# First two pairs of the up projection without the seven-product scheme, and another order of reads in its last pair

## What is computed

```
m = rmsnorm(h, g_mlp)
h = h + square(relu(m @ w_up)) @ w_down        # 1024 -> 4096 -> 1024
```

## Time and profile before

| | us |
|---|---|
| median of 3 runs | 4737.99 (4730.15 to 4739.12) |
| time of the profiled execution | 4743.6 |
| its span, first to last instruction | 4741.8 |
| PE busy in it | 4288.3 |
| first up phase, from its first load to pair 2 | 77.8 |
| second up phase, the same stretch | 78.9 |

### The profile page before, as it was taken

The page is one execution under the profiler, slowest core; times in us unless marked ns, Lnnn a source line. Parts: engine busy times, 40 slices in busy tenths (PEclk is TensorE's granted clock), DMA queues, the critical chain, the costliest instruction groups (busy, mean ns, idle before and its releaser), DMA issues. The chain is left out here.

```text
span 4741.8 us, 67334 instructions
## 1 busy us (share of the span) xinstructions
PE 4288.3 (90%) x28381; PEld 3484.5 (73%) x28381; DVE 2114.8 (45%) x2906; ACT 1598.6 (34%) x2680; POOL 633.2 (13%) x514
## 2 busy tenths in 40 slices
PE   7988899987979979899998799999989778899998
PEld 5988889756958858677435588788767676787887
DVE  4544426363245552324443566433442363765333
ACT  3632234342243332311675333222332333433221
POOL 0024400010001100002231232000100002221001
PEclk8999999998989989999999899999999898999999
DMA  3110012122110021111001132431111211234222
GB/s 111 38 60 2 2 45 67 47 64 80 44 36 9 9 75 48 63 40 45 32 9 31 55 111 107 143 97 58 53 33 42 65 40 42 92 112 151 82 91 71
DMA packets 320899, 284.92 MB, mean 60 GB/s; under 512 B 19505, under 2 KB 286033, under 8 KB 320482
## 3 DMA queue, kind: packets, MB, share of 16 engines
q1 hardware_dynamic: 320610, 280.76, 19.0%
HBM read 204.55 MB, written 55.31 MB: 55 GB/s over the span
## 5 line engine op out<-in xcount | busy, mean ns | idle before, releaser
L3063 PE MATMUL ff_bank<-ff_x_hi_rounded,ff_wh_rounded 128*128 128x512 f32 x896 | 361.3, 403 | 56.8 <-DVE ff_wl_rounded L3226 37.3
L3081 PE MATMUL ff_acc<-ff_x_hi_rounded,ff_wh_rounded 128*128 128x512 f32 x1024 | 398.3, 389 | 0.0
L3081 PE MATMUL ff_acc<-ff_x_hi_rounded,ff_wl_rounded 128*128 128x512 f32 x1024 | 398.3, 389 | 0.0
L3081 PE MATMUL ff_acc<-ff_x_rounded,ff_wh_rounded 128*128 128x512 f32 x1024 | 398.3, 389 | 0.0
L3063 PE MATMUL ff_bank<-ff_x_hi_rounded,ff_wl_rounded 128*128 128x512 f32 x896 | 357.8, 399 | 0.0
L3063 PE MATMUL ff_bank<-ff_x_rounded,ff_wh_rounded 128*128 128x512 f32 x896 | 357.2, 399 | 0.0
L3063 PEld LDWEIGHTS ff_bank<-ff_x_hi_rounded,ff_wh_rounded 128*128 128x128 f32 x896 | 173.6, 194 | 106.1 <-DVE ff_wl_rounded L3226 45.5
L3125 ACT ACTIVATE ff_wh_rounded<-ff_wl 128x512 fp32r<-128x512 f32 x128 | 80.8, 632 | 418.8 <-DMA ff_wl<-w_down_dram 208.2
L3081 PEld LDWEIGHTS ff_acc<-ff_x_rounded,ff_wh_rounded 128*128 128x128 f32 x1024 | 192.2, 188 | 40.1
L3081 PEld LDWEIGHTS ff_acc<-ff_x_hi_rounded,ff_wh_rounded 128*128 128x128 f32 x1024 | 192.2, 188 | 40.0
L3081 PEld LDWEIGHTS ff_acc<-ff_x_hi_rounded,ff_wl_rounded 128*128 128x128 f32 x1024 | 192.2, 188 | 39.6
(11 more groups left out here) (623 smaller groups left out, 10421.7 us busy)
## 6 DMA issues: line engine op xcount, KB each, us to landing
inner<-ff_made_out SPq DMA_DIRECT2D x64, 512.0 KB, 2.6
ff_x<-inner SPq DMA_DIRECT2D x64, 512.0 KB, 5.5
ff_raw<-w_up_dram SPq DMA_DIRECT2D x32, 512.0 KB, 4.1
ff_wl<-w_down_dram SPq DMA_DIRECT2D x64, 256.0 KB, 3.1
ff_raw<-w_mlp_dram SPq DMA_DIRECT2D x32, 512.0 KB, 4.2
ff_wl<-w_mlp_dram SPq DMA_DIRECT2D x64, 256.0 KB, 3.0
mid_w<-w_in_dram SPq DMA_DIRECT2D x104, 128.0 KB, 2.6
pa_w<-w_in_dram SPq DMA_DIRECT2D x72, 128.0 KB, 2.6
```

The source lines that it names most:

```text
L3063: mm = M(to, rounded(a[:, j, h, :]), rounded(b[:, j, h, :]), start=(j in (0, 1, 5) and h == 0 and i == 0), stop=(h == H - 1 and i == 2), s ...
L3081: mm = M(acc[:, s, c, :], rounded(a[:, s, k, :]), rounded(b[:, at, c * W2:(c + 1) * W2]), start=(k == 0 and i == 0), stop=(k == KD - 1 and ...
```

## The change

Pairs 0 and 1 (`PLAIN` = 2) are made in the ordinary form: four steps `u`, each one weight block against two input blocks of 512 tokens, 24 matmuls, so 96 matmuls a pair instead of 84. They need no combinations, so POOL leaves `combine(0)` and `combine(1)` out, and the input blocks 0, 1, 5 and 6 alone: ACT writes each high part straight from `hid` with the gain, 1024 elements at once, and DVE makes the low part from `hid` in one instruction. The first pair's weights come in four DMAs of 256 KB instead of two of 512 KB. The four combinations are made during pairs 0 and 1, from scaled copies that `scale_x` writes: blocks 4, 2 and 3 by POOL in nine subtractions (eight of 512 elements, then one of 2048), block 1 by DVE in one of 2048 (`t3`, which lies in `square`). They are split (`high_t`, `low_t`) at the start of pair 2, the first in the seven-product form. In the last pair `read(LAST, 1)` and `read(LAST, 2)` come ahead of `high_y(0)` on ACT, and DVE's reads and `shape` are placed differently among its `low_y`.

```diff
--- before.py
+++ after.py
...
+    PLAIN, SLOT = 2, (0, 5, 6, 3)
...
+        t3 = square[:, :, :].rearrange("p s (h n) -> p (s h) n", n=W2)
+        products = lambda q: 4 * min(q, PLAIN) + J * max(q - PLAIN, 0)
+        act_reads = lambda q: 2 * min(q, PLAIN) + 4 * max(q - PLAIN, 0)
+        dve_reads, sums_made = lambda q: 3 * max(q - PLAIN, 0), lambda q: 4 * max(q - PLAIN, 0)
+        first_half = lambda q: 0 if q < PLAIN else 1
+        plain_acc = {(0, 0): acc[:, 1], (0, 1): bank[:, 0:2], (1, 0): bank[:, 2:4], (1, 1): acc[:, 0]}
...
+                cols = q * 2 * P
+                if q == 0:
+                    for u in range(4):
+                        ks, f = slice(u % 2 * H, (u % 2 + 1) * H), u // 2
+                        sp.dma_start(raw[:, ks, f * P:(f + 1) * P], up_view[:, ks, f * P:(f + 1) * P]).then_inc(raw_first[u], 16)
+                    return
+                if q <= PLAIN:
+                    sp.wait_ge(w_low, products(q))
+                else:
+                    sp.wait_ge(w_low, products(q - 1) + 6)
+                    sp.wait_ge(combined, sums_made(q))
...
+                store(q, first_half(q))
                 if q + 2 < PAIRS:
                     load_pair(q + 2)
-                store(q, 0)
+                store(q, 1 - first_half(q))
...
+            def multiply_plain(q, u):
+                to, j, blocks = plain_acc[q, u // 2], SLOT[u], (0, 1) if u % 2 == 0 else (5, 6)
+                pe.wait_ge(w_low, products(q) + u + 1)
+                if (q, u) == (1, 2):
+                    pe.wait_ge(act_read, 1)
+                for h in range(H):
+                    if q == 0 and u < 2:
+                        pe.wait_ge(x_low, u * H + h + 1)
+                    for c in range(C2):
+                        for i, (a, b) in enumerate(((wh, x_hi), (wl, x_hi), (wh, x))):
+                            mm = M(to[:, c, :], rounded(a[:, j, h, :]), rounded(b[:, blocks[c], h, :]),
+                                   start=(u % 2 == 0 and h == 0 and i == 0), stop=(u % 2 == 1 and h == H - 1 and i == 2))
+                mm.then_inc(product, 1)
...
+                if j == 0:
+                    pe.wait_ge(act_read, act_reads(q - 1))
...
+                    pe.wait_ge(act_read, act_reads(q) + 2)
...
+                if q == PLAIN and j in (1, 2, 3, 4):
+                    pe.wait_ge(t_low, {4: 1, 2: 2, 1: 3, 3: 4}[j])
...
+            def high_plain(q, u):
+                if q == 0:
+                    act.wait_ge(raw_first[u], 16)
+                else:
+                    act.wait_ge(product, products(q - 1) + u + 1)
+                    act.wait_ge(raw_in[u % 2], 16 * q)
+                A(rounded(wh[:, SLOT[u]]), plain_source[u], ACT.Copy).then_inc(w_high, 1)
...
+            def high_x(k):
+                at = slice(0, 2) if k < H else slice(5, 7)
+                A(rounded(x_hi[:, at, k % H, :]), cut(hid[:, k, :]), ACT.Copy, scale=gain[:, k:k + 1]).then_inc(x_high, 1)
+
+            def scale_x(h):
+                A(x_hi[:, 2:4, h, :], cut(hid[:, h, :]), ACT.Copy, scale=gain[:, h:h + 1]).then_inc(scaled, 1)
+                lower, g = cut(hid[:, h + H, :]), gain[:, h + H:h + H + 1]
+                A(x_hi[:, 4, h, :], lower[:, 1, :], ACT.Copy, scale=g).then_inc(scaled, 1)
+                A(x[:, 3, h, :], lower[:, 0, :], ACT.Copy, scale=g).then_inc(scaled, 1)
+
+            def high_t(t, j, what):
+                if j == 1:
+                    act.wait_ge(summed_x, 1)
+                    act.wait_ge(product, products(1) + 3)
+                else:
+                    act.wait_ge(third, 2 * H if j != 3 else 2 * H + 1)
+                    act.wait_ge(summed_x, 1)
+                A(rounded(x_hi[:, j]), what, ACT.Copy).then_inc(t_high, 1)
+
+            def copy(q, i):
+                act.wait_ge(product, products(q) + 2 * (i + 1))
+                A(cut(made_out[:, q % 2, i, :]), plain_acc[q, i], ACT.Copy).then_inc(act_read, 1)
...
+            for u in range(2):
+                high_plain(0, u)
+                for h in range(H):
+                    high_x(u * H + h)
+            high_plain(0, 2)
+            high_plain(0, 3)
+            scale.root(act)
+            copy(0, 0)
             for h in range(H):
-                A(x[:, 5:7, h, :], cut(hid[:, h + H, :]), ACT.Copy, scale=gain[:, h + H:h + H + 1]).then_inc(x_scaled, 1)
-                act.wait_ge(x_made, 2 * h + 1)
-                A(rounded(x_hi[:, 0, h, :]), x[:, 0, h, :], ACT.Copy).then_inc(x_high, 1)
-            high(0, 1)
-            high_x(1)
-            scale.root(act)
-            read(0, 0)
-            for j in range(2, J):
-                high(0, j)
-                high_x(j)
-                if j in (2, 3):
-                    read(0, j - 1)
-            for j in range(J - 1):
-                high(1, j)
-            read(0, 6)
-            high(1, 6)
-            for q in range(1, LAST):
+                scale_x(h)
+            high_plain(1, 0)
+            high_plain(1, 1)
+            copy(0, 1)
+            high_plain(1, 2)
+            high_plain(1, 3)
+            copy(1, 0)
+            high(PLAIN, 0)
+            high_t(0, 4, x[:, 4])
+            high_t(1, 2, x[:, 2])
+            high(PLAIN, 1)
+            high_t(2, 1, t3)
+            high_t(3, 3, x[:, 3])
+            high(PLAIN, 2)
+            copy(1, 1)
+            for j in range(3, J):
+                high(PLAIN, j)
+            for q in range(PLAIN, LAST):
...
-            read(LAST, 0)
+            for j in range(3):
+                read(LAST, j)
             high_y(0)
             high_y(1)
-            read(LAST, 1)
             high_w(0)
-            read(LAST, 2)
             for i in range(2, 6):
                 high_y(i)
             high_w(1)
+            read(LAST, 6)
             high_y(6)
             high_y(7)
-            read(LAST, 6)
...
-            combine(0)
             for h in range(H):
-                pool.wait_ge(x_made, 2 * h + 2)
-                pool.wait_ge(x_scaled, h + 1)
-                T(x[:, 1, h, :], x[:, 6, h, :], x[:, 1, h, :], ALU.subtract).then_inc(third, 1)
-            for q in range(1, PAIRS):
+                pool.wait_ge(scaled, 3 * h + 2)
+                T(x[:, 4, h, :], x_hi[:, 3, h, :], x_hi[:, 2, h, :], ALU.subtract).then_inc(third, 1)
+                pool.wait_ge(third, 2 * h + 1)
+                T(x[:, 2, h, :], x_hi[:, 4, h, :], x[:, 4, h, :], ALU.subtract).then_inc(third, 1)
+            pool.wait_ge(scaled, 3 * H)
+            pool.wait_ge(third, 2 * H)
+            T(x[:, 3], x[:, 3], x[:, 2], ALU.subtract).then_inc(third, 1)
+            for q in range(PLAIN, PAIRS):
...
+            def low_x(k):
+                at = slice(0, 2) if k < H else slice(5, 7)
+                dve.wait_ge(x_high, k + 1)
+                V.scalar_tensor_tensor(rounded(x[:, at, k % H, :]), cut(hid[:, k, :]), gain[:, k:k + 1], rounded(x_hi[:, at, k % H, :]),
+                                       ALU.mult, ALU.subtract).then_inc(x_low, 1)
+
+            def low_t(t, j, what):
+                dve.wait_ge(t_high, t + 1)
+                if j == 2:
+                    dve.wait_ge(third, 2 * H + 1)
+                T(rounded(x[:, j]), what, rounded(x_hi[:, j]), ALU.subtract).then_inc(t_low, 1)
...
+            for u in range(2):
+                low_plain(0, u)
+                for h in range(H):
+                    low_x(u * H + h)
+            low_plain(0, 2)
+            low_plain(0, 3)
+            shape(0, 0)
+            low_plain(1, 0)
+            low_plain(1, 1)
+            dve.wait_ge(scaled, 3 * H)
+            T(t3, x_hi[:, 4], x_hi[:, 3], ALU.subtract).then_inc(summed_x, 1)
             shape(0, 1)
-            for j in range(5):
-                low(1, j)
-            read(0, 5)
-            low(1, 5)
-            low(1, 6)
-            shape(0, 0)
-            for q in range(1, LAST):
+            low_plain(1, 2)
+            low_plain(1, 3)
+            shape(1, 0)
+            low(PLAIN, 0)
+            low_t(0, 4, x[:, 4])
+            low_t(1, 2, x[:, 2])
+            low(PLAIN, 1)
+            low_t(2, 1, t3)
+            low_t(3, 3, x[:, 3])
+            low(PLAIN, 2)
+            shape(1, 1)
+            for j in range(3, J):
+                low(PLAIN, j)
+            for q in range(PLAIN, LAST):
...
+            read(LAST, 3)
+            read(LAST, 4)
             low_y(0)
             low_y(1)
             low_w(0)
+            read(LAST, 5)
             low_y(2)
-            read(LAST, 3)
-            low_y(3)
-            read(LAST, 4)
             shape(LAST, 1)
-            low_y(4)
-            read(LAST, 5)
-            low_y(5)
+            for i in range(3, 6):
+                low_y(i)
             low_w(1)
+            shape(LAST, 0)
             low_y(6)
             low_y(7)
-            shape(LAST, 0)
             for m in range(TILES):
                 g, f, s = m // G, m % G, m % 2
                 if g >= 1 and f == 0:
```

140 lines of the change are left out of this document (56 added, 84 removed).

## The result

The changed kernel takes 4705.24 us (median of 5, 4700.76 to 4709.98) against 4738.27 (4730.15 to 4747.08): ratio 0.9931, 95% interval 0.9917 to 0.9945, a gain of 33 us with an interval of 26 to 39. The forecast was 4711, a gain of 27.

A forecast was written before the change was run, and what follows sets the result against it. PE, busy 4288 of 4742 us, was taken as the bound, with time to win in its gaps and slow clock. Gains 10.7 + 2.6 + 11.8 + 1.8 = 26.9 gave a median of 4711 us, range 4701 to 4722.

The forecast's parts named there:

- Start, pairs 0 and 1: From the first load through pairs 0 and 1: pair 2 begins at 55.2 us instead of 77.8, 22.6 gained.
- The low clock: Start of pair 0: half clock for 5.2 us of work, costing 2.5 us (bounds 1.7 to 3.4).
- The two waits: PE stops in pair 1: 1.1 us at its start, 2.0 us ahead of step 2.
- Pair 2: Pair 2 gives part back through two waits, ending at 86.1 against 96.85: gain 10.7 us, second feed-forward 11.8.
- the whole hold: In pair 1 `shape(0, 1)` stands still for all of POOL's 2048-element subtraction; PE waits 2.0 us.
- 1.1 a time: In pair 1 DVE loses at most 1.1 us for each instruction beside POOL; PE would wait 0.4 us.
- The two chains: In pair 2 product 1 waits 3.6 us for `t3`'s split, product 3 3.5 for `read(2, 1)` behind pair 3's load.
- Seam: Last pair's product 2 to second down tile: gain 2.6 us (3.8 to 1.3), second feed-forward 1.8.
- (b): Pair 2 stops ahead of nearly every product, losing 17 us, with another stop of 3 in pair 3; 4727 us, 11%.
- (c): Clock stays at 0.50 through all of pair 2, so the change gains only 2 us; 4736 us, 7%.
- (d): Clock doesn't rise in the plain pairs, losing 8 us a feed-forward; 4754 us, 4%.
- (a): DVE and POOL hardly meet in pair 2 and its clock stays up; 10 us more gained, 4701 us, 8%.

The follow-up runs named there:

- e3: Changed kernel with GpSimd's one subtraction of 2048 elements cut into four of 512; 4704.3 us, ratio 0.9936.
- e7: Changed kernel with `shape(1, 1)` moved behind the last weight split of pair 2 on VectorE; 4693.2 us, ratio 0.9909.
- e4: Changed kernel with the last pair's second shape put back behind the splits of tiles 6 and 7 on VectorE; 4699.1 us, ratio 0.9927.
- e1: Changed kernel with the old seam, so only the start is changed; 4712.2 us, ratio 0.9951 against the kernel before.
- e2: Kernel before the change with only the new seam; 4734.9 us, ratio 0.9992.
- e11: Changed kernel with one more float32 matmul of 512 columns, result unused, ahead of the sum over features; 4706.1 us, ratio 0.9930.
- e12: e10 with one more matmul ahead of the sum over features; 4680.3 us, ratio 0.9868.
- e10: e9 with e4's edit, input combinations split in the order 2, 1, 3, 4 and `high(PLAIN, 2)` moved; 4676.4 us, ratio 0.9870.
- e6: Changed kernel with pair 2's ScalarE reads 0 to 2 and VectorE's two reads ahead of pair 3's weight splits; 4700.2 us, ratio 0.9921.
- e9: e8 with early reads on ScalarE in pairs 2 and 3 and on VectorE, there in pair 3 behind two weight splits; 4687.7 us, ratio 0.9890.
- e8: Changed kernel with `shape(1, 1)` behind pair 2's weight splits and input combinations split in the order of use; 4702.7 us, ratio 0.9928.

## Why the prediction was right

The forecast is in brackets.

**Start, pairs 0 and 1.** First product at 6.06 (forecast 6.0), half clock for 5.7 (5.2), step 1 of pair 0 at 1.00. The low clock cost step 0 2.8 us (2.5). No row had stood behind the bounds of 1.7 to 3.4 for this term; over all runs without the added matmul it cost 0.1 to 3.0, by where the clock rose. The two waits are 1.08 (1.1) and 1.21 (2.0), `shape(0, 1)` took 5.62 (about 5). Step 2 of pair 1 began at 44.3, as forecast; its wait was shorter because pair 0 had ended 0.5 later. Pair 2 begins at 55.3 (55.2). The gain of the start is that of its parts together (the ordinary form, the input split straight from `hid`, the loads in four); no run took them apart. The choice of the whole hold over 1.1 a time was right: the three rows under e3 fit only an exclusion that lasts the whole instruction, in both directions. The Trainium skill (SBUF — State Buffer, "Who interferes with whom") says the same; by that rule this trace agrees, with 4.4 us lost in one instruction.

**Pair 2.** The two chains came as laid out: the low part that product 1 needs ended at 61.5 (forecast 61.5), pair 3's load was issued at 68.5 (68.5), and `read(2, 1)` ended at 73.5 (73.3). Product 1 waited 3.45 (3.6) and took 4.1 (5.2); product 3 waited 4.60 (3.5), with "issue" for its releaser and not L3174, and took 4.3 (4.6). The ends differ less than the parts: 86.0 against 86.1, because the start of product 3 is fixed by VectorE's last splits and the load of pair 3, which e7 showed, and not by what PE lost before it. Gain 10.8 (10.7). In the second feed-forward 9.8 (11.8), although pair 2 began at 55.3 again: two terms of pair 2 were mis-sized, since I carried the first start over. Product 3 began 0.9 later (74.5 against 73.6), since pair 3's load was issued 0.5 later and ScalarE's split behind it came another 0.4 later. And the clock cost more: products 1 and 3 took 4.4 and 5.3 us, most of both at half clock, and the pair ended at 88.1.

**Seam.** Products 3 to 6 ran through, to +10.9; the wait at tile 6 was 2.63 (3.4), the second tile began at +25.0 (25.3 to 27.8): gain 4.1 (2.6, at most 3.8), in the second 2.0 (1.8). VectorE's part of tile 6 was ready at +22.1 (22.6), TensorE wanted it at +19.5 (19.2), and the clock stayed up behind the wait in the first feed-forward. e4 showed that VectorE's order was the cause of the wait.

**Sum.** 10.8 + 9.8 + 4.1 + 2.0 = 26.7, forecast 26.9. The mechanism was right, but a fit to 0.2 us is luck: 2.0 too little in the second pair 2 stands against 1.5 too much in the first seam, and both hang on where the clock rose or fell. e1 bore out the start's half, e2 the seam's roughly. The median's other 6 us are not explained by the change. The profiled executions differ by 42.8 in span, of which 16.3 lie in code that is the same; a gain of 26.5 is just inside the median's interval (26 to 39). The median less S is 3982 to 3994 us over the fourteen kernels, and the kernel before (3991) and the changed one (3985) both lie within that spread, so nothing shows the other 6 us to be the change's. What makes the rest vary was not looked into.

**Rivals.** (b) needed stops before nearly every product of pair 2 and a further one in pair 3: there were two, and pair 3 ran at clock 1.00. (c) and (d) needed low clock through pair 2 or through the plain pairs: their windows show 0.89 (pair 2 of the second feed-forward 0.84). Of (a), the engines did meet: all of the first four DVE splits of pair 2 were stretched.

## What to carry to other kernels

Of two waits on one engine, only the one whose chain ends last sets the time: clear it first, measure, and then try again the edits that paid nothing before (the order of the splits paid nothing alone and 4 us a feed-forward once the reads stood ahead of the next pair's weights). When a wait's releaser reads "issue", or names an instruction that ended long before, look at the queue in which the releasing instruction stands, and at what stands ahead of it: a read of PSUM behind an instruction that waits for a load holds the matmuls until that load has landed. Judge edits worth a few us by stretches of the profile that hold them, not by the median of the whole program, and take off what the clock gave or took by chance in the same stretch: count from the beginning of the pair, not from the first load.

## What the runs showed of the hardware

VectorE and GpSimd, both reading two inputs from SBUF, excluded each other for whole instructions, and the row of the one that waits starts when it would have begun: GpSimd's 6.46 us were 2.0 of waiting and 4.45 of work. Cut into four, they took turns, with 1.1 lost to VectorE each time, as much in all.

TensorE's clock was up at its first product when float32 matmuls of the sum had kept it busy from 5.8 to 6.0 us before it on, with one pause of 0.6 to 0.9 (e11, e12, four times of four). With four such rows and a pause of 2.0 to 2.3 it was up in two of twenty. Waits of 1.3 in pair 2 left it at 1.00 (e10), waits of 3.5 and 3.9 brought it down; waits between 1.9 and 2.7 did both. Ahead of product 3 of pair 3 in e6, a wait of 1.94 us was followed by a granted clock of 0.61 over that product in the first feed-forward, and one of 2.01 by 1.00 in the second. At depth tile 6 of the first down tile of the changed kernel the window shows 1.00 in the first feed-forward and 0.89 in the second, for 2.63 and 2.62 us of waiting. In pair 2 a wait of 2.64 left it at 1.00 (first feed-forward of e9), and one of 2.54 was followed by a product of 4.4 us instead of 2.7 (e8).
